# Prompt heads start four half tiles earlier in eight steps, and key pages stay out of the steps between two projections

## The reference: one layer of a hybrid decoder

```python
def hybrid_layer(x, prev_pool, prev_conv, prev_ffn, attn_fn, ...):
    xn = rms_norm(x, norm1_g)
    proj = xn @ w_in                                   # 2048 -> 5128 columns
    u_pool, h_b, h_c, h_x, q, k, v, f_logit = jnp.split(proj, [...], axis=-1)
    y_pool, pool_state = causal_pool_mix(u_pool, prev_pool, pool_w, pool_scale)
    conv_out, conv_state = causal_dwconv(h_c * h_x, prev_conv, conv_w)
    y_conv = h_b * conv_out
    q = rms_norm(q.reshape(b, t, N_HEADS, HEAD_DIM), q_norm_g)
    k = rms_norm(k.reshape(b, t, N_HEADS, HEAD_DIM), k_norm_g)
    v = v.reshape(b, t, N_HEADS, HEAD_DIM)
    logf = jax.nn.log_sigmoid(f_logit + b_f)
    y_att = attn_fn(q, k, v, logf)                     # 8 heads of 128, causal, with a forget bias
    g_pool, g_conv, g_att = jnp.split(out_norm_g, [...])
    mix = jnp.concatenate([rms_norm(y_pool, g_pool), rms_norm(y_conv, g_conv), rms_norm(y_att, g_att)], axis=-1)
    x = x + mix @ w_o
    xn2 = rms_norm(x, norm2_g)
    a, gate = jnp.split(xn2 @ w_up, 2, axis=-1)
    a_conv, ffn_state = causal_dwconv(a, prev_ffn, ffn_conv_w)
    x = x + (jax.nn.silu(a_conv + ffn_conv_b) * gate) @ w_down
    return x, pool_state, conv_state, ffn_state, k, v, logf
```

## Time and profile before

| | us |
|---|---|
| median of 3 runs | 2841.31 |
| lowest and highest | 2840.59, 2846.02 |
| the profiled execution | 2837.32 |
| its span, from the first to the last instruction | 2835.7 |
| mean granted clock of TensorE in it | 0.953 of full |
| busy: PE, DVE, ACT, POOL | 2607.2, 1424.3, 737.4, 169.4 |

### The profile page before, as it was taken

The page is one execution under the profiler, slowest core; times in us unless marked ns, Lnnn a source line. Parts: engine busy times, 40 slices in busy tenths (PEclk is TensorE's granted clock), DMA queues, the critical chain, the costliest instruction groups (busy, mean ns, idle before and its releaser), DMA issues.

```text
span 2835.7 us, 50766 instructions
## 1 busy us (share of the span) xinstructions
PE 2607.2 (92%) x19729; PEld 2336.7 (82%) x19729; DVE 1424.3 (50%) x5630; ACT 737.4 (26%) x1029; POOL 169.4 (6%) x343
## 2 busy tenths in 40 slices
PE   6878898898985599979999999999999999999998
PEld 3777677777773255549999999999999999999998
DVE  5787776767655942234434343434343434343433
ACT  5222123333431311133222222222222222222221
POOL 0100111111112121200000000000000000000000
PEclk8888989999997799989999999999999999999999
DMA  8678999998989697753222222222222222222221
GB/s 298 219 253 313 353 332 338 341 350 314 360 287 341 220 371 247 267 178 119 90 90 90 90 90 90 90 90 90 93 101 99 96 90 90 90 90 90 90 90 64
DMA packets 272564, 524.03 MB, mean 185 GB/s; under 512 B 16535, under 2 KB 182268, under 8 KB 271012
## 3 DMA queue, kind: packets, MB, share of 16 engines
q1 hardware_dynamic: 218717, 365.71, 37.4%
q0 software_dynamic: 40304, 142.46, 13.7%
q10 hardware_dynamic: 13303, 12.62, 1.3%
HBM read 501.58 MB, written 17.50 MB: 183 GB/s over the span
## 4 chain that ended last, share of the span: by engine, by line
PE 61%; DMA 2%; DVE 2%; issue 1%; ACT 1%; POOL 0%; POOLq 0%; DVEq 0%; ACTq 0%
PE ps L740 61%; DMA t_r<-in_cache_v 1%; DMA t_wraw<-in_w_o 1%; DVE t_xl L1681 1%; DVE t_r L1852 0%; DVE t_stg L1737 0%; PE ps L743 0%; DVE t_wl L1681 0%; ACT t_xh L1267 0%; DVE t_work L1681 0%; DVE t_stg L2024 0%; ACT t_wh L1267 0%; POOL out_conv_prompt L539 0%; POOL out_conv_sample L539 0%; POOLq L542 0%
## 5 line engine op out<-in xcount | busy, mean ns | idle before, releaser
L740 PE MATMUL ps<-t_xh,t_wh 128*128 128x260 f32 (+1 forms) x4352 | 1078.3, 299 | 36.4 <-DVE t_wlr L1681 21.4
L740 PE MATMUL ps<-t_xl,t_wh 128*128 128x260 f32 (+1 forms) x4352 | 1051.1, 293 | 0.0
L740 PEld LDWEIGHTS ps<-t_xh,t_wh 128*128 128x128 f32 x4352 | 743.3, 192 | 169.5 <-issue 116.2
L1267 ACT ACTIVATE t_wh<-t_wraw 128x1024 fp32r<-128x1024 f32 x376 | 398.5, 1060 | 1465.9 <-PE ps L740 1392.0
L1681 DVE TENSOR_TENSOR t_wl<-t_wraw,t_wh 128x1024 fp32r<-128x1024 f32 x296 | 362.4, 1225 | 824.9 <-ACT t_wh L1267 824.9
L740 PEld LDWEIGHTS ps<-t_xl,t_wh 128*128 128x128 f32 x4352 | 742.5, 192 | 10.2 <-issue 1.2
L740 PE MATMUL ps<-t_xh,t_wl 128*128 128x260 f32 (+1 forms) x3072 | 676.9, 293 | 0.0
L1852 DVE CUSTOM_DVE_ANT_0 t_r<-t_r,t_work 128x128 f32<-128x128 f32 x2048 | 455.0, 287 | 205.0 <-DMA t_r<-in_cache_k 188.5
L740 PEld LDWEIGHTS ps<-t_xh,t_wl 128*128 128x128 f32 x3072 | 487.4, 189 | 12.0
L740 PE MATMUL ps<-t_xh,t_wlr 128*128 128x260 f32 x1280 | 374.1, 292 | 0.0
L740 PE MATMUL ps<-t_hh,t_wh 128*128 128x260 f32 x1408 | 283.0, 282 | 3.4 <-issue 3.4
(11 more groups left out here) (305 smaller groups left out, 1250.2 us busy)
## 6 DMA issues: line engine op xcount, KB each, us to landing
t_r<-in_cache_k SPq DMA_DIRECT2D x256, 512.0 KB, 6.5
t_r<-in_cache_v POOLq DMA_DIRECT2D x256, 512.0 KB, 6.7
t_wraw<-in_w_up SPq DMA_DIRECT2D x44, 2048.0 KB, 8.0
t_wraw<-in_w_down SPq DMA_DIRECT2D x22, 2048.0 KB, 7.7
t_wraw<-in_w_in SPq DMA_DIRECT2D x21, 2048.0 KB, 14.2
t_wraw<-in_w_o SPq DMA_DIRECT2D x11, 2048.0 KB, 11.3
scr_x<-t_r POOLq DMA_DIRECT2D x1, 4160.0 KB, 20.0
t_work<-in_x_prompt SPq DMA_DIRECT2D x4, 1024.0 KB, 6.6
```

The source lines that it names most:

```text
L740: return pe.matmul(out, lhsT, rhs, start=start, stop=stop)
L1267: return act.activation(out, in_, ACT.Copy)
```

## The change

- `HEAD0` is 28 instead of 32, `STAGES` 8 instead of 7. Step 0 on PE is empty. The keys now go into rows first (at 3) and the values second (at 4), on PE and ACT. The sum of squares of step 1 goes to bank 3. ACT's square of the previous head's output is in step 2, DVE's sum of it in 3. The transposes and the copies to `pT` are step 6, the product with the values step 7. DVE's normalising stays 5. Head h - 1 still ends while head h is in its steps 0 and 1. The last head ends at step 77 instead of 80, and its output is stored and loaded again as the others' are (14 tiles in `load_y`).
- The first 8 pages of a sample come four to a step, so a sample takes 10 steps. Steps 80 to 83 have no key page. Before step 80 stand 250 key pages instead of 227 (96 instead of 88 of them before step 32), in steps 84 and 85 the last six. The last value page is in step 109 instead of 111; the gap has 16 value pages instead of 14, and from step 84 on there are 84 instead of 88.
- SP waits for the y loads ahead of step 84's key pages.
- In the gap the order is: step 80 total of the heads on PE, convolution and the last sums on DVE; 81 conv rows and the convolution's total on PE, the four weight rests and the samples' squares on DVE; 82 and 83 four mixing pairs each.
- The stores of samples' rows go in one DMA where the rows allow it, 15 instead of 32; the last eight are at step 92 instead of 87. `kSn` lies the other way round in its buffer, and the samples' values are copied beside it.
- The end of a step on PE: the heads' part comes behind all but the last value pages, the transposes no longer last of all.

```diff
-HEAD0 = 32
-STAGES = 7
+HEAD0 = 28
+STAGES = 8
@@ page_slots
-            take = min(3, PAGES - done)
+            if CHUNKS <= at < OUT0:
+                at = OUT0
+            take = min(4 if done < 8 else 3, PAGES - done)
@@ sample_store
+                if n in (0, 2, 3):
+                    pool.dma_start(dst, src).then_inc(r_stored, 16)
+                    return
+                for g in range(CONV_T):
+                    size = dst.shape[1]
...
-                for n in {18: (0, 1), OWN_K + 11: (2, 3), CHUNKS + 7: (4, 5)}.get(s, ()):
+                for n in {18: (0, 1), OWN_K + 11: (2, 3), CHUNKS + 12: (4, 5)}.get(s, ()):
@@ block.sync
                 kp = KEYS.get(s, [])
+                if s == OUT0:
+                    sp.wait_ge(y_loaded, 32)
@@ block.tensor, head
-                if stage == 0:
-                    rows_of(h, 0)
                 if stage == 1:
                     pe.wait_ge(h_sq, h + 1)
                     if h:
-                        pe.wait_ge(h_done, h)
                         pe.wait_ge(h_pC, 4 * h)
+                        pe.wait_ge(h_rowsC, 2 * h)
...
-                    mm(ps[:, 6, :], ones[:, :], sqs[:, 0, :])
+                    mm(ps[:, 3, :], ones[:, :], sqs[:, 0, :])
...
                     last.then_inc(h_S, 1)
+                    rows_of(h, 0)
+                if stage == 4:
                     rows_of(h, 1)
-                if stage == 5:
+                if stage == 6:
                     pe.wait_ge(h_pn, h + 1)
-                    pe.wait_ge(h_e, h + 1)
...
-                if stage == 6:
+                if stage == 7:
                     pe.wait_ge(h_pC, 4 * h + 4)
-                    pe.wait_ge(h_rowsC, 2 * h + 1)
+                    pe.wait_ge(h_rowsC, 2 * h + 2)
@@ block.tensor, the steps
-                at_head = head_stages(s)
-                value_pages(late[:2])
-                for h, stage in at_head:
-                    if stage != 5:
-                        head(h, stage)
+                if s == CHUNKS:
+                    pe.wait_ge(h_pC, 4 * HEADS)
+                    mix_total(2, 14, msum[2], 2)
                 if s == CHUNKS + 1:
                     conv_rows()
-                if s == CHUNKS + 2:
-                    pe.wait_ge(h_done, HEADS)
-                    mix_total(2, 14, msum[2], 2)
                     mix_total(1, 16, msum[1], 5)
+                value_pages(late[:2])
+                for h, stage in head_stages(s):
+                    head(h, stage)
...
-                for h, stage in at_head:
-                    if stage == 5:
-                        head(h, stage)
@@ block.scalar, load_y
-                act.wait_ge(y_stored, 16 * 13)
+                act.wait_ge(y_stored, 16 * 14)
                 act.dma_start(ymix[:, 0:6, 0:SEQ], scry[0:6].rearrange("k p t -> p k t")).then_inc(y_loaded, 16)
-                act.dma_start(ymix[:, 8:15, 0:SEQ], scry[6:13].rearrange("k p t -> p k t")).then_inc(y_loaded, 16)
+                act.dma_start(ymix[:, 8:16, 0:SEQ], scry[6:14].rearrange("k p t -> p k t")).then_inc(y_loaded, 16)
@@ block.vector, the steps
+                if s == CHUNKS - 1:
+                    mix_sum(13)
+                if s == CHUNKS:
+                    mix_sum(14)
+                    mix_sum(15)
                 if s == CHUNKS + 1:
-                    for n in range(13, 16):
-                        mix_sum(n)
-                    mix_pair(0)
-                    mix_pair(2)
-                if s == CHUNKS + 2:
                     dve.wait_ge(h_O, HEADS)
                     dve.wait_ge(h_stored[1], 16 * HEADS)
-                    weight_rest(0, CHUNKS)
-                    weight_rest(0, CHUNKS + 1)
-                    weight_rest(0, CHUNKS + 2)
-                    weight_rest(0, CHUNKS + 3)
-                    dve.wait_ge(r_stored, 384)
+                    dve.wait_ge(y_stored, 16 * 14)
+                    for c in range(4):
+                        weight_rest(0, CHUNKS + c)
+                    dve.wait_ge(r_stored, 112)
                     sample_squares(0, 8)
+                if s == CHUNKS + 2:
+                    for t in range(0, 8, 2):
+                        mix_pair(t)
                 if s == CHUNKS + 3:
-                    for t in range(4, 16, 2):
+                    for t in range(8, 16, 2):
                         mix_pair(t)
```

105 lines of the change are left out of this document (55 added, 50 removed).

## The result

The changed kernel takes 2800.24 us in the median of 4 runs (2798.29 to 2802.78), the kernel before 2840.95 beside it; the ratio is 0.9856, with a 95% interval of 0.9839 to 0.9873. So the change gains 41 us, on the forecast side, but just over half of the 76 that the sum gave: 2765 was forecast, the range 2732 to 2808.

What follows compares the result with a forecast made beforehand. VectorE fills the early half tiles, PE the heads (with stalls for VectorE's normalising) and output, nobody the gap. Terms +9 - 35 - 42 - 8 = -76 took 2837.3 to 2761.3, plus 4.0 carried over: 2765 us, range 2732 to 2808.

Steps and rivals of the forecast that it cites:

- Part 1: Heads: transposes one half tile later, so six stalls for VectorE's normalising (35.4 us) go or fall under 2 us each.
- Part 2, before step 32: Eight more key pages before step 32 lose 9 us, bounds 0 and 15.
- five of the eight, times 1.78: Before step 32: five early pages cost their 1.78 us of scoring, 9 us lost; nothing for the other three.
- lie in PE's waits: Head 0's sums, mask and scores, now in steps 29 to 31, fall in PE's waits for weight rests.
- Part 2, steps 32 to 79: Head stretch: twelve cycles of four half tiles shorten and gain 35 us, bounds 0 and 55.
- the cycle of 39.5 us: Steps 32 to 79: 14.9 MB at 377 GB/s, against 42.4 us before, 37.8 undisturbed and VectorE's 31.7 of work.
- Rival (a): DMA at 359 GB/s bounds the heads: cycle 41.5 us, gain there 11, total -52, 2789 us; chance 0.23.
- the rule of the Trainium skill: Counter-rule: at 358 GB/s a cycle can't be under 41.6 us, so the heads would gain 10 us, not 35.
- it is wrong if weight issues stay 42 us apart: Sign against the forecast in the heads, which expected weight issues 39.5 us apart on average.
- Part 3: Gap: y landed at +28, sample product at +62 instead of 103.7; gain 42 us, bounds 26 and 50.
- Part 4: Output: residual-load stall gone 7, four value pages fewer 2, row stores minus 1; gain 8 us, bounds 0 and 14.
- The slower rival (c): Late key pages behind weight loads make PE wait for weight rests: cycle 47.6 us, total +21, 2862 us; chance 0.07.

Runs made afterwards that it cites:

- e3: Kernel before with only the new page table and SyncE's wait for y, old heads, gap order and stores: 2835.72 us, ratio 0.997.
- e6: Changed kernel with four key pages a step only for samples 3 to 7, so 88 pages before step 32: 2784.69 us, ratio 0.979.
- e14: Changed kernel with VectorE's weight rest ahead of a step's first key page: 2793.22 us, ratio 0.984.
- e8: Changed kernel with 88 key pages before step 32, the other 168 in steps 32 to 79, residual loads in step 86: 2802.13 us, ratio 0.985.
- e2: Changed kernel with the page table of before, three key pages a step, steps 80 to 83 included: 2813.87 us, ratio 0.989.
- e12: Changed kernel with a quarter of each key page loaded and half the heads scored, scores not the reference's: 2715.4 us.
- e5: Changed kernel with four of eight heads of each key page scored from the second sample on: 2754.4 us.
- e4: Changed kernel with only a quarter of each key page loaded, from the fifth page on: 2750.7 us.
- e7: Changed kernel without SyncE's wait for y ahead of step 84: 2799.95 us, ratio 0.984.
- e9: Changed kernel with its three large residual loads in step 90 instead of 86: 2799.32 us, ratio 0.984.

## Why the prediction was right in sign and half wrong in size

**Part 1, the stalls at the transposes: right.** Under 10 us was asked, 4.0 is left. e3 shows the other side: without the later stages the same page table makes them 48.1.

**Part 2, before step 32: the step "five of the eight, times 1.78" failed**, and with it the bound of 15. The price of a page was taken as its scoring. Measured are 2.55 us a page if all eight count alike (e3), 20.4 us in all against 9 forecast, and 24.1 (e6) and 27.6 (e14) in two other settings; the moved heads, put at nothing because they "lie in PE's waits", cost 1 to 4 (e6, e8, e2). The two value pages and the parts of the softmax that come forward with the key pages were left out of the sum, and so was the clock, which the text's own part on the stalls does price.

**Part 2, steps 32 to 79: the step that failed is the cycle of 39.5 us.** PE's floor was right (37.7 in e12), the rate of 377 GB/s was attainable (375 over the whole stretch in e5), and VectorE's 31.7 us do fit under either. What was wrong is to take the largest of three separate times as the cycle. Transfers and VectorE lengthen it together (e4, e5, e12; that the four buffers couple them is the likely way and not shown), and the cycle is 1.8 us above 39.5, 22 us in twelve. Rival (a) had 41.5 us and 2789 in total and comes nearer, but not by its reason: transfers are not held to 359 GB/s, as e5 shows. Nor is the rule of the Trainium skill ("DMA: Bandwidth & Descriptors", section Specifications, about 358 GB/s a core) the cause, although its 41.6 us look like a hit: 375 GB/s in e5 over 470 us and 391 in the gap stand above it. Two causes gave the same number, and only the run that relieves the other engine tells them apart. The sign "it is wrong if weight issues stay 42 us apart" was nearly met, with 41.3.

**Part 3: right, 5 us too good.** The sample product came at +67.0 instead of +62: y 3 us later than +28, the stretch behind the last pair 2 to 3 longer. The 27 us of idling ahead of the convolution are gone as said. SyncE's wait, used to get +28, has no part in it (e7). What was named as a side condition, no page ahead of the convolution, is 29.8 of the 36.7 us (e3).

**Part 4: right in sign, for the wrong reason.** Forecast 8, bound 14, measured 15.8. The stall at the residual loads was to give 7; their place gives nothing (e9): the 3.5 us stall of the earlier trace rows is gone in the changed kernel, and in e9, with the loads late, as well. 12.5 us come from the last value page, step 109 instead of 111, which the front of this document tells; the sum had 2 us for the four pages fewer and nothing for the end of the output. These 8 us above the forecast are luck: without them the total would stand at the range's upper end, 2808.

**The slower rival (c)** did not come: waits for weight rests in steps 32 to 79 are 1.0 us. Its mechanism lives before step 32, where the longest such wait grew from 6.4 to 10.2 us.

## What to carry to other kernels

Where a queue of transfers and an engine feed each other through a few buffers, the busy time of each may fit into a cycle and the cycle still be longer than both: relieve each alone and both together before one is called the bound. Work moved out of a gap has to be paid where it goes, at a price that grows with how full that place already is (here 0.7 to 1.0 us a page up to some 153, 1.9 above, 2.5 and more in the first steps, and none that could be measured for nine key pages in the output): so move it to the later, emptier steps. And what stands first behind a wait should be what needs the wait; putting the weight rest ahead of the key page was worth 20 us for two exchanged lines where the early steps had room, and 7 where they were full.

## What the runs showed of the hardware that was not expected

Transfers held 375 GB/s at a share of 1.01 for 470 us (e5), while ordinary stretches of the same program ran at 353 with a share of 0.97. In the head stretch a few short waits cost PE as much again in clock: 25.5 us idle in 15 waits went with a mean of 0.95 and a busy time of 470.6 us, 3.3 us idle in three with 0.99 and 448.8, for the same matmuls. Longer waits did not cost more: 42.0 us idle in 9 waits (the kernel before) went with 0.95 and 467.2.
